# Two of 256 gathers of expert rows, each made in two transfers (120 rows and 8 rows)

## The chip, the cores and the metric

One core of one Trainium2 chip runs the whole program in one launch. The metric is the device time of a launch in microseconds, the median over several runs.

## What is computed

`x` has 256 tokens of 1024 channels. Two transformer stacks run one after the other in float32. The first has two layers (a gated mixer with neighbourhood and context attention, a convolution block, and squared-ReLU MLPs); the second has one layer: a mixer of two kinds of attention and then a feed-forward part with product-key experts. The change touches the last part, whose reference is, cut short:

```python
def peer_ffn(h, w_query, sub_keys, u_emb, v_emb):
    q = (hc @ w_query).reshape(B, T_CHUNK, PEER_HEADS, 2, PEER_DKEY // 2)
    s = jnp.einsum('bthpd,hpnd->bthpn', q, sub_keys)
    s_top, i_top = lax.top_k(s, PEER_TOPK)
    ...
    g_s, pos = lax.top_k(cand, PEER_TOPK)
    e_idx = jnp.take_along_axis(cand_idx, pos, axis=-1)
    g = jax.nn.softmax(g_s, axis=-1)
    u = u_emb[e_idx]
    act = jax.nn.gelu(jnp.einsum('btd,bthkd->bthk', hc, u), approximate=False)
    return jnp.einsum('bthk,bthkd->btd', g * act, v_emb[e_idx])
```

There are 8 heads and 16 chosen experts per head out of 16384, so each token needs 128 rows of `u_emb` and 128 of `v_emb`. The output is `x` plus this result times a gate row, with a final RMS norm.

## The kernel before

The program is written by hand for five engines, with semaphores; each engine runs its own list. VectorE is DVE, ScalarE is ACT, TensorE is PE, GpSimd is POOL and SyncE is SP in the profile.

**Gathers.** `u_emb` and `v_emb` lie side by side in one tensor `in_uv`, so that one expert is one row of 2048 floats, 8 KB. The 256 tokens are two halves of 128 (`n`), a token per partition. Gather number `g` brings one row for each of the 128 tokens of a half: half `g // 128`, head `g % 128 // 16`, choice `g % 16`. Two successive gathers are a lot (`LOTS`, `l = g // 2`), and there are 128 lots. `gather(l)` (lines 1810 to 1822) is GpSimd's list: it waits until the experts of the head are known (`s_eu`), and before each gather until the mix of the row that last used the buffer is done (`s_mix`), then issues one indirect DMA with 128 indices, one per partition, from `eu[:, h, k]` (a part of `crow`). The buffers are 10 for the first 80 gathers and 14 after that (`row_of`, line 491): two parts of `row_x`, `HID`, `row_w`, `row_h` each and six of `ring`. Every buffer has its semaphore (`s_row`), and `row_turn` (line 492) gives its value when gather `g` has landed, 16 for each transfer. From gather 84 on, gather `g` reuses the buffer of `g - 14`.

**Consumers.** For each row VectorE makes the dot with the token's `h` (`dot(l)`, line 1261, 1024 elements per partition, written over the `u` half). ScalarE takes the gelu of the two dots of a lot (line 1695), multiplies by the gates (1699) and makes two diagonal matrices (1705). TensorE adds `diag x v` to a sum in PSUM, four matmuls a row (`mix(l)`, line 2318; two calls of a 512-column matmul, each run as two). For the last two lots gelu and diagonal are made row by row (lines 1712 and 1269). Beside the dots VectorE makes the routing of later heads, 16 steps (`route_steps`; the list of experts is written at line 1245, which increments `s_eu`). Step `r` is half `r // 8` and head `r % 8`.

**End.** `finish(0)` closes the first half after lot 65, and SyncE stores output rows 0 to 127 (line 2456). `finish_last()` closes the second half, with the stores at lines 2458 and 2460.

**Elsewhere.** In the convolution block VectorE clears two borders of `yp` and waits for them with the semaphore `s_pad` (lines 896 to 898).

Of the kernel before, what the change touches and what calls it, by code (L numbers as in the profile page):

```python
# [7 lines left out]
U32 = mybir.dt.uint32  # L8
# [71 lines left out]
def program(nc, A, out):  # L80
    es = ExitStack()
    with es:
# [3 lines left out]
        def sem(name):  # L86
            return es.enter_context(nc.semaphore(name))
# [100 lines left out]
        ef = af[:, 1760:1792].rearrange("p (s k) -> p s k", s=2)  # L188
        e1 = af[:, 1792:1808]
        eu = af[:, 1808:1936].bitcast(U32).rearrange("p (h k) -> p h k", h=8)  # L190
        gates_ = On[:, 0:128].rearrange("p (h k) -> p h k", h=8)
        dots = On[:, 128:256].rearrange("p (h k) -> p h k", h=8)
        wts = On[:, 256:384].rearrange("p (h k) -> p h k", h=8)
# [120 lines left out]
        def unit_src(i):  # L314
            if not in_ring(i):
                return (late[:, 0:1024], late[:, 1024:2048], bias[:, 3072:4096], ring[:, pair_slot(L0 + 4), 0:1024])[i - W0 - 12]
            return ring[:, pair_slot(i // 2), i % 2 * 1024:i % 2 * 1024 + 1024]
# [67 lines left out]
        relu_h = Steps(sem("act_relu_hi"), [(l, s, m) for l in range(2) for s in range(8) for m in range(4)])  # L385
        relu_l = Steps(sem("dve_relu_lo"), [(l, s, m) for l in range(2) for s in range(8) for m in range(4)])
        CV, CP = (0, 1, 2, 3, 4), (5, 6, 7)
        s_pad, s_diag, s_tap, s_mean, s_cen = sem("dve_pad"), sem("act_diag"), sem("pe_tap"), sem("pe_mean"), sem("dve_centred")
        y_v, y_a = Steps(sem("dve_conv"), CV), Steps(sem("act_conv"), CP)
        s_ln, s_silu, s_yh, s_yl = sem("dve_ln"), sem("act_silu_y"), sem("act_y_hi"), sem("dve_y_lo")  # L390
        TAPS = [(kt, k) for kt in CP for k in range(31)]
# [5 lines left out]
        s_scp, s_sc2 = sem("pe_key_score"), sem("act_key_score")  # L397
        s_ngr, s_rge, s_eu = sem("dve_route_max"), sem("act_route_exp"), sem("dve_route")
        s_eu8 = sem("dve_route_first_eight")
        s_row = [sem(f"row{i}_in") for i in range(14)]  # L400
        s_dot, s_gate, s_dg, s_mix = sem("dve_dot"), sem("dve_gate_share"), sem("act_mix_diag"), sem("pe_mix")
        s_ms, s_msr, s_y, s_out = sem("dve_ms"), sem("act_ms_root"), sem("dve_y"), sem("out_done")
# [86 lines left out]
                      or 35 <= l < 40 or l >= 40 and l % 8 < 5]  # L489
        chosen_at = {route_lots[5 * (r - 1) + 2] + 1: r for r in range(1, 16)}  # L490
        row_of = [g % 10 if g < G1 else (g - G1 + 10) % NROW for g in range(256)]
        row_turn = [row_of[:g + 1].count(row_of[g]) for g in range(256)]
        row_prev = [max([p for p in range(g) if row_of[p] == row_of[g]], default=None) for g in range(256)]

        def row_in(g):
# [3 lines left out]
        row_ap = []  # L499


        def dve():
# [390 lines left out]


            have_mod(1, 2)
            ve.memset(yp[:, :, 0:15], 0.0).then_inc(s_pad, 1)
            ve.memset(yp[:, :, 271:286], 0.0).then_inc(s_pad, 1)
            V.wait_ge(s_pad, 2)
            V.then_inc(ve.tensor_tensor(ab[:, 4, :], M[:, 1, 16:24], col["bpw2"], ALU.mult))
            r = rstd("conv")  # L900
            V.wait_ge(affined.sem, affined.n)
# [864 lines left out]
        def pool():  # L1766
# [43 lines left out]
            def gather(l):  # L1810
                n, h, k0 = LOTS[l]
                if l < 4:
                    G.wait_ge(s_eu8, 1)
                else:
                    G.wait_ge(s_eu, 8 * n + h + 1)
                for i in range(2):
                    g = 2 * l + i
                    if row_prev[g] is not None:
                        G.wait_ge(s_mix, row_prev[g] + 1)
                    sm, _ = row_in(g)  # L1820
                    nc.gpsimd.indirect_dma_start(row_ap[row_of[g]], None, A["uv"],  # L1821
                                                 bass.IndirectOffsetOnAxis(ap=eu[:, h, k0 + i:k0 + i + 1], axis=0)).then_inc(sm, 16)

            G.wait_ge(s_mod, NM)
            gather(0)
# [558 lines left out]
        def sync():  # L2384
# [63 lines left out]
            for i in (L0, L0 + 1, L0 + 4):  # L2448
                for j in (2 * i, 2 * i + 1):
                    P.wait_ge(*dense[used[j]])  # L2450
                if i < L0 + 2:
                    pair(i + 4)
                else:
                    sp.dma_start(unit_src(W0 + 15), A["stream"][L0 + 7][:, 1024:2048]).then_inc(s_late[2], 16)
            P.wait_ge(s_y, 1)
            sp.dma_start(out[0, 0:128, :], xN[:, 0, :]).then_inc(s_out, 16)
            P.wait_ge(s_y, 2)
# [101 lines left out]
```

## Time and profile before

| | |
|---|---|
| median of 3 runs | 1540.09 us |
| lowest and highest | 1537.85 and 1541.22 us |
| the profiled execution's own time | 1538.54 us |
| its span, first to last instruction | 1537.2 us |
| mean granted TensorE clock | 0.992 |
| TensorE busy | 1377.1 us (90%) |
| VectorE busy | 1190.0 us (77%) |
| ScalarE busy | 721.2 us (47%) |
| GpSimd busy | 335.7 us (22%) |
| gathers: software queue | 36864 packets, 268.45 MB |

The span is shorter than the execution's own time by 1.3 us, which lie around it. Times in views are counted from the span's start. The DMA share is the mean busy share of the core's 16 DMA engines; neighbouring packets of an engine overlap a little in the records, so it can read 1.01. The name `P` in the rows is the buffer of the diagonals, `On` holds dots, weights and gates, and `cT` holds the tokens' `h`.

### The profile page before, as it was taken

What the parts mean: (1) busy time and instruction counts of PE and PEld (TensorE: products, weight loads), DVE (VectorE), ACT (ScalarE), POOL (GpSimd) and SP (SyncE); (2) the same over time, 40 slices, a digit from 0 to 9 for tenths busy, and PEclk for the clock granted to TensorE, in tenths of its full rate; (3) what the DMA queues carried; (4) which work ended last, traced back from release to release, by engine and by line L of the source; (5) the groups of instructions that cost most, each with busy time, mean ns of one, the idle gap of its engine ahead of it and who ended that gap; (6) DMA issues with size and microseconds to landing.
All of it is one profiled execution on the core that took longest, in us unless ns stands there. A gap on an engine that the chain in (4) does not pass through costs nothing.

```text
span 1537.2 us, 20250 instructions
## 1 busy us (share of the span) xinstructions
PE 1377.1 (90%) x7314; PEld 1007.4 (66%) x7314; DVE 1190.0 (77%) x2398; ACT 721.2 (47%) x1636; POOL 335.7 (22%) x312
## 2 busy tenths in 40 slices
PE   8999999999999999998999999999887687777776
PEld 3878899999997999998888844444332232223222
DVE  6977888887997788887787687777877777667655
ACT  4555565556486645555354443434433233333322
POOL 1100100001000000003110343445644254434430
PEclk9999999999999999999999999999999999999999
DMA  9764369997520499993432699999999999999995
GB/s 390 314 233 165 138 249 360 353 359 295 196 107 27 152 343 366 344 332 135 165 110 86 233 423 421 421 421 421 420 423 420 423 421 422 421 421 421 421 421 221
DMA packets 66341, 477.12 MB, mean 310 GB/s; under 512 B 7361, under 2 KB 7361, under 8 KB 9153
## 3 DMA queue, kind: packets, MB, share of 16 engines
q0 software_dynamic: 36864, 268.45, 42.0%
q1 hardware_dynamic: 29376, 207.37, 36.2%
q8 instruction: 58, 0.95, 0.2%
q14 instruction: 41, 0.34, 0.1%
q10 hardware_dynamic: 2, 0.01, 0.0%
HBM read 474.75 MB, written 1.05 MB: 310 GB/s over the span
## 4 chain that ended last, share of the span: by engine, by line
PE 52%; DMA 29%; DVE 11%; ACT 5%; issue 2%; POOL 1%; DVEq 0%; ACTq 0%; POOLq 0%
DMA ring<-in_uv,crow 11%; DMA row_x<-in_uv,crow 8%; PE ps L2318 6%; PE ps L1872 6%; PE ps L1874 5%; PE ps L1873 5%; DMA HID<-in_uv,crow 5%; PE ps L2189 4%; PE ps L2192 4%; PE ps L2191 4%; PE ps L2216 3%; PE ps L2331 2%; DVE WB L533 2%; DMA row_h<-in_uv,crow 2%; PE ps L1905 1%
## 5 line engine op out<-in xcount | busy, mean ns | idle before, releaser
L533 DVE TENSOR_TENSOR WB<-ring,WB 128x1024 fp32r<-128x1024 f32 x208 | 256.9, 1238 | 54.0 <-ACT WB L1345 51.7
L1345 ACT ACTIVATE WB<-ring 128x1024 fp32r<-128x1024 f32 x208 | 218.4, 1052 | 125.9 <-PE ps L2192 87.0
L1872 PE MATMUL ps<-hH,WB 128*128 128x256 f32 x752 | 216.6, 288 | 5.6 <-DVE WB L533 3.8
L2318 PE MATMUL ps<-ring,P 128*128 128x512 f32 x376 | 173.7, 607 | 46.5 <-ACT P L1705 46.5
L1873 PE MATMUL ps<-hL,WB 128*128 128x256 f32 x752 | 214.1, 285 | 0.0
L1874 PE MATMUL ps<-hH,WB 128*128 128x256 f32 x752 | 214.0, 285 | 0.0
L1695 ACT ACTIVATE On<-On 128x2 f32<-128x2 f32 x126 | 25.6, 203 | 369.5 <-DVE On L1261 369.4
L518 DVE CUSTOM_DVE_ANT_0 ring<-ring,crow,cols 128x1024 f32<-128x1024 f32 x128 | 163.5, 1279 | 21.1 <-DMA ring<-in_um 20.9
L2318 PEld LDWEIGHTS ps<-ring,P 128*128 128x128 f32 x376 | 68.9, 191 | 149.4 <-ACT P L1705 78.6
L1261 DVE CUSTOM_DVE_ANT_0 ring<-ring,cT 128x1024 f32<-128x1024 f32 x94 | 114.7, 1225 | 65.9 <-DMA ring<-in_uv,crow 64.0
L1872 PEld LDWEIGHTS ps<-hH,WB 128*128 128x128 f32 x752 | 145.6, 194 | 8.0 <-DVE WB L533 4.7
L2189 PE MATMUL ps<-XB,WB 128*128 128x256 f32 x512 | 145.1, 283 | 1.6 <-DVE WB L533 1.6
L1873 PEld LDWEIGHTS ps<-hL,WB 128*128 128x128 f32 x752 | 145.7, 194 | 0.1
L1874 PEld LDWEIGHTS ps<-hH,WB 128*128 128x128 f32 x752 | 145.6, 194 | 0.0
L2191 PE MATMUL ps<-XB,WB 128*128 128x256 f32 x512 | 144.9, 283 | 0.0
L2192 PE MATMUL ps<-XB,WB 128*128 128x256 f32 x512 | 144.9, 283 | 0.0
L1773 POOL TENSOR_TENSOR sq<-sq 128x256 f32<-128x256 f32 x30 | 29.3, 977 | 528.9 <-ACT sq L1350 526.9
L1821 POOL DMA_INDIRECT ring<-in_uv,crow x94 | 102.0, 1085 | 137.9 <-PE ps L2318 108.8
L2318 PE MATMUL ps<-row_w,P 128*128 128x512 f32 x160 | 75.6, 616 | 27.5 <-ACT P L1705 27.5
L2189 PEld LDWEIGHTS ps<-XB,WB 128*128 128x128 f32 x512 | 98.3, 192 | 2.0 <-DVE WB L533 2.0
L2192 PEld LDWEIGHTS ps<-XB,WB 128*128 128x128 f32 x512 | 98.3, 192 | 0.0
L2191 PEld LDWEIGHTS ps<-XB,WB 128*128 128x128 f32 x512 | 98.3, 192 | 0.0
(348 smaller groups left out, 2895.5 us busy)
## 6 DMA issues: line engine op xcount, KB each, us to landing
ring<-in_stream SPq DMA_DIRECT2D x114, 1024.0 KB, 6.7
ring<-in_um SPq DMA_DIRECT2D x66, 1024.0 KB, 7.5
ring<-in_wm SPq DMA_DIRECT2D x4, 1024.0 KB, 12.5
bias<-in_bias SPq DMA_DIRECT2D x2, 2048.0 KB, 15.4
HID<-in_um SPq DMA_DIRECT2D x4, 512.0 KB, 17.9
ring<-in_uv,crow POOLq DMA_INDIRECT x94, 27.6
xT<-in_xT SPq DMA_DIRECT2D x1, 1024.0 KB, 8.5
cT<-in_cxT SPq DMA_DIRECT2D x1, 1024.0 KB, 15.3
```

Of the source, the lines that this page charges most:

```text
L518: ve.tensor_tensor_reduce(wk, wk, crow[:, layer // 2, :], 1.0, col[f"bm{layer}"][:, m:m + 1], ALU.mult, ALU.add, M[:, layer, m:m + 1]).the ...
L533: ve.tensor_tensor(unit_dst(j, 1), unit_src(j), f(unit_dst(j, 0)), ALU.subtract).then_inc(s_lo, 1)
L1261: ins = ve.tensor_tensor_reduce(u, u, hN[:, n, :], 1.0, 0.0, ALU.mult, ALU.add, dots[:, h, k0 + i:k0 + i + 1])
L1345: se.activation(unit_dst(j, 0), unit_src(j), ACT.Copy).then_inc(s_hi, 1)
L1821: nc.gpsimd.indirect_dma_start(row_ap[row_of[g]], None, A["uv"], bass.IndirectOffsetOnAxis(ap=eu[:, h, k0 + i:k0 + i + 1], axis=0)).then_i ...
L1872: te.matmul(o, wh[:, c], hi[:, kt, :], start=(kt == 0), stop=False)
L1873: te.matmul(o, wh[:, c], lo[:, kt, :], start=False, stop=False)
L1874: mm = te.matmul(o, wl[:, c], hi[:, kt, :], start=False, stop=(kt == 7))
L2189: te.matmul(o, wh[:, c], rH[d % 2][:, k, :], start=(d == 0 and h == 0 and k == 0), stop=False, skip_group_check=True)
L2191: te.matmul(o, wh[:, c], rL[d % 2][:, k, :], start=False, stop=False, skip_group_check=True)
L2192: mm = te.matmul(o, wl[:, c], rH[d % 2][:, k, :], start=False, stop=(d == 7 and k == 3), skip_group_check=True)
L2318: mm = te.matmul(ps[4 + 2 * n + q][:, :], diag[:, g % 8, :], row_ap[row_of[g]][:, 1024 + q * 512:1536 + q * 512], start=(g % 128 == 0), st ...
```

## The change

Gathers 226 and 230 are both of the second half, head 6, choices 2 and 6, with buffers `row_x` and `row_w`. Each becomes two indirect DMAs into the same buffer: rows (partitions) 0 to 119 with their indices as before, then rows 120 to 127, whose indices are read from `eut`, on partitions 0 to 7. SyncE fills `eut` with one transfer of 8 x 16 indices from `eu[120:128, 6, :]`, once `s_eu` has reached 15. The buffer's semaphore counts 32 for such a gather. `eut` lies in a free part of `crow`. The new semaphore `s_eut` comes in, `s_pad` goes, and VectorE's own semaphore takes its place.

```diff
+        eut = af[0:8, 1936:1952].bitcast(U32)
...
-        s_pad, s_diag, s_tap, s_mean, s_cen = sem("dve_pad"), sem("act_diag"), sem("pe_tap"), sem("pe_mean"), sem("dve_centred")
+        s_diag, s_tap, s_mean, s_cen = sem("act_diag"), sem("pe_tap"), sem("pe_mean"), sem("dve_centred")
...
+        s_eut = sem("last_tokens_experts_in")
...
-        row_turn = [row_of[:g + 1].count(row_of[g]) for g in range(256)]
+        SPLIT = (226, 230)
+        row_turn = [sum((1 + (p in SPLIT)) * (row_of[p] == row_of[g]) for p in range(g + 1)) for g in range(256)]
...
-            ve.memset(yp[:, :, 0:15], 0.0).then_inc(s_pad, 1)
-            ve.memset(yp[:, :, 271:286], 0.0).then_inc(s_pad, 1)
-            V.wait_ge(s_pad, 2)
+            V.then_inc(ve.memset(yp[:, :, 0:15], 0.0))
+            V.then_inc(ve.memset(yp[:, :, 271:286], 0.0))
+            V.wait_own()
...
                     sm, _ = row_in(g)
-                    nc.gpsimd.indirect_dma_start(row_ap[row_of[g]], None, A["uv"],
-                                                 bass.IndirectOffsetOnAxis(ap=eu[:, h, k0 + i:k0 + i + 1], axis=0)).then_inc(sm, 16)
+                    n_tok = 120 if g in SPLIT else 128
+                    nc.gpsimd.indirect_dma_start(row_ap[row_of[g]][0:n_tok, :], None, A["uv"],
+                                                 bass.IndirectOffsetOnAxis(ap=eu[0:n_tok, h, k0 + i:k0 + i + 1],
+                                                                           axis=0)).then_inc(sm, 16)
+                    if g in SPLIT:
+                        G.wait_ge(s_eut, 16)
+                        nc.gpsimd.indirect_dma_start(row_ap[row_of[g]][120:128, :], None, A["uv"],
+                                                     bass.IndirectOffsetOnAxis(ap=eut[:, k0 + i:k0 + i + 1], axis=0)).then_inc(sm, 16)
...
+            h_split = SPLIT[0] % 128 // 16
+            P.wait_ge(s_eu, 8 + h_split + 1)
+            sp.dma_start(eut, eu[120:128, h_split, :]).then_inc(s_eut, 16)
             P.wait_ge(s_y, 1)
             sp.dma_start(out[0, 0:128, :], xN[:, 0, :]).then_inc(s_out, 16)
```

GpSimd's list around gathers 224 to 231, before; `pe_mix` is the wait for a buffer's last mix, `dve_route` the wait for a head's experts, and each row is one gather (x2 two alike):

```order
L1821 DMA ring<-in_uv,crow 128x2048 [waits pe_mix,dve_route]
L1821 DMA ring<-in_uv,crow 128x2048 [waits pe_mix]
L1821 DMA row_x<-in_uv,crow 128x2048 [waits pe_mix] x2
L1821 DMA HID<-in_uv,crow 128x2048 [waits pe_mix] x2
L1821 DMA row_w<-in_uv,crow 128x2048 [waits pe_mix] x2
```

And in the changed kernel:

```order
L1825 DMA ring<-in_uv,crow 128x2048 [waits pe_mix,dve_route]
L1825 DMA ring<-in_uv,crow 128x2048 [waits pe_mix]
L1825 DMA row_x<-in_uv,crow 120x2048 [waits pe_mix]
L1830 DMA row_x<-in_uv,crow 8x2048 [waits last_tokens_experts_in]
L1825 DMA row_x<-in_uv,crow 128x2048 [waits pe_mix]
L1825 DMA HID<-in_uv,crow 128x2048 [waits pe_mix] x2
L1825 DMA row_w<-in_uv,crow 120x2048 [waits pe_mix]
L1830 DMA row_w<-in_uv,crow 8x2048
L1825 DMA row_w<-in_uv,crow 128x2048 [waits pe_mix]
```

The first of the two gathers into `row_x` and the first of those into `row_w` are now a large and a small transfer each, with the gathers behind them in their old order; the first small one also waits for `eut`.

SyncE's list at the end, before, where the first row is the last load of weights and the others store the output:

```order
L2454 DMA ring<-in_stream 128x1024 [waits pe_dense]
L2456 DMA out<-xN 128x1024 [waits dve_y]
L2458 DMA out<-xN 128x512 [waits dve_y]
L2460 DMA out<-xN 128x512 [waits act_last_y]
```

And in the changed kernel:

```order
L2463 DMA ring<-in_stream 128x1024 [waits pe_dense]
L2466 DMA crow<-crow 8x16 [waits dve_route]
L2468 DMA out<-xN 128x1024 [waits dve_y]
L2470 DMA out<-xN 128x512 [waits dve_y]
L2472 DMA out<-xN 128x512 [waits act_last_y]
```

The copy of the indices and its wait for `s_eu` (`dve_route`) stand ahead of the store of the first half.

## Rows read from the trace of the kernel before

**Rows 1.** Page: busy time, the span in 40 slices, DMA queues.

```profile
PE 1377.1 (90%) x7314; PEld 1007.4 (66%) x7314; DVE 1190.0 (77%) x2398; ACT 721.2 (47%) x1636; POOL 335.7 (22%) x312
...
GB/s 390 314 233 165 138 249 360 353 359 295 196 107 27 152 343 366 344 332 135 165 110 86 233 423 421 421 421 421 420 423 420 423 421 422 421 421 421 421 421 221
...
q0 software_dynamic: 36864, 268.45, 42.0%
...
q8 instruction: 58, 0.95, 0.2%
```

**Rows 2.** Busy time by stretch: us, engines' busy time (instructions), clock, DMA share, GB/s.

```profile
880.00:980.00 100.00, 92.25 (x282) 49.71 (x280) 75.23 (x199) 42.30 (x123) 43.38 (x40) 1.00 1.01 422
...
1400.00:1500.00 100.00, 73.64 (x160) 28.55 (x159) 58.30 (x122) 30.54 (x104) 40.61 (x40) 1.00 1.01 421
```

**Rows 3.** Timeline of VectorE: first dots of two successive lots.

```profile
1444.96 1.23 DVE L1261 CUSTOM_DVE_ANT_0 ring<-ring,cT 128x1024 f32<-128x1024 f32 x1 [1.37 <-DMA ring<-in_uv,crow]
...
1449.94 1.23 DVE L1261 CUSTOM_DVE_ANT_0 ring<-ring,cT 128x1024 f32<-128x1024 f32 x1 [1.37 <-DMA ring<-in_uv,crow]
```

**Rows 4.** Groups by line, 1440 to 1519 us, VectorE's dots and TensorE's mixes.

```profile
L1261 DVE CUSTOM_DVE_ANT_0 ring<-ring,cT 128x1024 f32<-128x1024 f32 x16 | 19.6, 1225 | 20.0 <-DMA ring<-in_uv,crow 20.0
...
L2318 PE MATMUL ps<-ring,P 128*128 128x512 f32 x56 | 25.9, 605 | 9.0 <-ACT P L1705 9.0
```

**Rows 5.** Chain of waits, 1480 us to the end: start, us, what.

```profile
1498.59 28.16 DMA row_x<-in_uv,crow
...
1533.96 0.72 ACT xN L1725
```

**Rows 6.** The end by stretch, columns as in rows 2.

```profile
1510.00:1515.00 5.00, 3.72 (x10) 1.45 (x9) 2.48 (x5) 1.38 (x5) 0.00 (x0) 1.00 1.01 419
...
1516.00:1517.00 1.00, 1.00 (x4) 0.41 (x3) 0.05 (x1) 0.00 (x0) 0.00 (x0) 1.00 0.64 270
...
1518.00:1519.00 1.00, 0.15 (x1) 0.00 (x0) 0.18 (x2) 0.72 (x4) 0.00 (x0) 1.00 0.22 90
...
1520.00:1521.00 1.00, 1.00 (x4) 0.52 (x3) 0.73 (x3) 0.20 (x1) 0.00 (x0) 1.00 0.08 33
...
1522.00:1523.00 1.00, 1.00 (x4) 0.42 (x3) 1.00 (x2) 0.00 (x0) 0.00 (x0) 1.00 0.06 25
...
1524.00:1525.00 1.00, 1.00 (x3) 0.39 (x3) 0.57 (x1) 0.00 (x0) 0.00 (x0) 1.00 0.06 25
```

**Rows 7.** Timeline of VectorE, dots of rows 254 and 255, a diagonal between.

```profile
1524.43 1.23 DVE L1261 CUSTOM_DVE_ANT_0 row_x<-row_x,cT 128x1024 f32<-128x1024 f32 x1 [0.73 <-DMA row_x<-in_uv,crow]
...
1525.93 0.35 DVE L1269 TENSOR_SCALAR P<-ident,On 128x128 f32<-128x128 f32 x1 [0.27 <-ACT On L1712]
1526.78 1.22 DVE L1261 CUSTOM_DVE_ANT_0 row_x<-row_x,cT 128x1024 f32<-128x1024 f32 x1 [0.50 <-DMA row_x<-in_uv,crow]
```

**Rows 8.** Timeline of VectorE, two dots around 1433 us.

```profile
1431.44 1.27 DVE L1261 CUSTOM_DVE_ANT_0 row_w<-row_w,cT 128x1024 f32<-128x1024 f32 x1 [0.96 <-DMA row_w<-in_uv,crow]
...
1435.00 1.23 DVE L1261 CUSTOM_DVE_ANT_0 row_h<-row_h,cT 128x1024 f32<-128x1024 f32 x1 [0.27 <-DMA row_h<-in_uv,crow]
```

**Rows 9.** Timeline of TensorE, one lot of mixes.

```profile
1504.49 3.70 PE L2318 MATMUL ps<-row_w,P 128*128 128x512 f32 x8 [1.27 <-ACT P L1705]
```

**Rows 10.** Timeline of GpSimd: gathers 226 and 230.

```profile
1426.24 1.38 POOL L1821 DMA_INDIRECT row_x<-in_uv,crow  x1 [1.45 <-PE ps L2318]
...
1436.22 0.94 POOL L1821 DMA_INDIRECT row_w<-in_uv,crow  x1 [1.89 <-PE ps L2318]
```

**Rows 11.** Timeline of VectorE: the fifteenth list of experts.

```profile
1394.44 0.17 DVE L1245 CAST crow<-crow 128x16 uint32<-128x16 f32 x1
```

**Rows 12.** The output's stores: issue, and from issue to landing.

```profile
L2456 SPq DMA_DIRECT2D out<-xN x1: 348/348/348, 1220.4 to 1220.4; - x1
...
DMA to landing us min/median/max: 2.0/2.3/7.6
```

**Rows 13.** VectorE's line 899, the add behind the memsets.

```profile
L899 DVE TENSOR_TENSOR ab<-M,cols x1: 168/168/168, 380.2 to 380.2; 128x8 f32<-128x8 f32 x1
```

## The prediction

> **What bounds the kernel now.** I start with the page. TensorE is busy for 90% of the span, but that is an average over two different stages: from slice 24 of 40 on, at about 884 us, the transfer rate stands at 420 to 423 GB/s in every slice but the last [rows 1], and between 1400 and 1500 us TensorE is down to 73.64 of 100 [rows 2]. This is the stage of the gathers; they are the software queue's 36864 packets, 268 MB of the 477 MB. Then the busy time by stretch: 421 or 422 GB/s and a DMA share of 1.01 early, and again at 1400 to 1500 us, so all 16 DMA engines work without a pause [rows 2]. One gather is 128 rows of 8 KB, 1.049 MB, or 2.49 us at 421 GB/s; the 256 of them are 637 us of the 1537.2. The dots show the same beat: first dots of successive lots start at 1444.96 and 1449.94 us, 4.98 us for two gathers [rows 3].
>
> The engines that consume the rows are not the limit. Between 1440 and 1519 us VectorE waits for landings before its dots: 20.0 us in front of the 16 dots on ring rows alone [rows 4]. TensorE, with 605 ns per matmul in this view and four matmuls per row, idles 9.0 us before the ring group [rows 4]. In the chain of waits the end hangs on the last row's DMA, from its issue at 1498.59 us for 28.16 us; behind it come one dot, one mix and the closing steps, up to 1537.2 [rows 5].
>
> The decisive view is the DMA share, microsecond by microsecond, at the end [rows 6]. Until 1515 us it is 1.01. Then it falls: 0.64 between 1516 and 1517, 0.22 between 1518 and 1519, 0.08 between 1520 and 1521, and 0.06 from 1522 to 1525. One engine of 16 is 0.0625: so most engines finish their share of row 255 by 1519, a second-slowest at about 1521, and **one engine works alone for more than 5 us**, until about 1526.5. A row counts as landed only when every engine has delivered, so this one sets the dot of row 255 at 1526.78. Its last rows come at the usual beat (dots at 1524.43 and 1526.78, 2.35 us apart [rows 7]): it isn't slow at the end, it is behind. Where it fell behind shows in one place: a dot at 1431.44 is followed by one at 1435.00, 3.56 us where the beat is 2.49 [rows 8]. The page has 58 instruction packets of 16 KB on another queue (0.95 MB) [rows 1]; I take it that these pass through a particular engine and push it back about 1 us each time, which would make the lag a property of the program and not of one run. That is an inference.
>
> **The change, part by part.** (a) Gathers 226 and 230 are split into rows 0 to 119 and 120 to 127. If 120 rows are dealt 8 to an engine, 15 engines get work and one gets none. If that one is the late engine, it saves 8 rows twice, 16 x 2.49/8 = 16 x 0.311 = 4.98 us. The 36864 packets are 144 per gather, 16 more than its rows [rows 1]; for what such extra packets of the two added transfers cost I take off 0.1: **-4.9 us** at its end, 1526.5 to 1521.6. (b) The eight odd rows are dealt one each to eight engines, 0.31 us per split. These engines don't decide unless they are close to the new end: the second-slowest finishes by about 1521 and would come to 1521.6 with two added rows. So the relief is just used up, and a third split would bring next to nothing. The sum takes -4.9.
>
> Is a consumer late next? To use 4.9 us TensorE must catch up: a lot is 8 matmuls, 3.70 us of the 4.98 us beat [rows 9], so 1.28 us can be regained per lot, and four lots make 4.9 us good. From row 226 to row 255 there are 15 lots. In the last four rows dot, gelu, scaled diagonal and mix chain one another: dot start 1524.43 to diagonal end 1526.28 is 1.85 us, less than the beat of 2.49 [rows 7]. Row reuse isn't short either: the last gather is issued at 1498.59 [rows 5], and no engine has finished it before 1515 [rows 6], so over 16 us of work stand queued at each.
>
> (c) GpSimd issues two more transfers. The order view shows each of them right behind its large one. An issue takes 0.94 to 1.5 us here; gather 226 is issued at 1426.24 and 230 at 1436.22 [rows 10], GpSimd is busy 40.6 of 100 us [rows 2], and a delay of gather 227 by 1.4 us is covered by the 16 us of queue. Cost 0; without that cover it would be 2 x 1.4 = 2.8 us. (d) The eight indices are copied from partitions 120 to 127 to partitions 0 to 7 by one SyncE transfer, which waits for the fifteenth step of routing, the cast at 1394.44 [rows 11]. The trace has no such small transfer; the nearest are the stores of 256 KB (2.0 us on idle engines at best) and of 512 KB in the middle of the gathers (7.6 us) [rows 12]. I take the upper, because this one too runs in full traffic: landed by 1402.2. It is needed behind gather 226's large part, at 1427.6: 25 us of slack, cost 0 between either bound. (e) SyncE's queue: behind that new wait stands the store of output rows 0 to 127, issued at 1220.36 now [rows 12]. It moves to about 1395. Its 0.52 MB are 1.25 us of all 16 engines at either place, nothing reads them on the chip, and the end comes 140 us later: 0. (f) The two memsets and the add behind them (the add takes 168 ns at 380.2 us [rows 13]) signal on VectorE's own semaphore instead of one of their own; both wait for the same two memsets: 0.
>
> **Sum.** The profiled execution took 1538.54 us for a span of 1537.2; 1538.54 - 4.9 = 1533.6. The median of the three runs is 1540.09, 1.55 above that execution and inside their spread of 1537.85 to 1541.22. Against the median: 1540.09 - 4.9 = **1535.2 us**. 0.2% is 3.1 us, about what a measurement of this kernel can tell from no change.
>
> **Rivals.** 1. *The late engine is not the one left out.* The trace doesn't number engines. Then it keeps its 8 rows and may be among those with an extra row: 0 to +0.6 us, 1540.1 to 1540.7. For it: nothing in the rows ties the late engine to the last partitions. Against it: there are only few natural places for an omission, first or last. The Trainium skill ("DMA: Bandwidth & Descriptors", "Latency and other measured facts") says that DMA engines 7 and 15 are usually slower than the rest, by a best guess because of the software queue's descriptor rings. An omission of the last engine would fit; but the beat here is the same for the late engine as for all, and what is seen is one engine behind, not two.
>
> 2. *The omission moves on from split to split.* If shares are dealt to engines from a running position, the 120 rows skip one engine, the 8 rows begin at just that engine, and the second split skips another one, seven places on. The late engine then saves 8 - 1 = 7 rows in one split and none in the other: 7 x 0.311 = 2.2 us, 1537.9. If it is never skipped, the case is rival 1. For it: the split into 15 and 8 shares is as natural as the fixed one. Against it: no row shows either. This is the rule of the Trainium skill ("DMA: Bandwidth & Descriptors", "Why a DMA increments its semaphore by 16 and not by 1"): the number of engines is the largest up to 16 that divides the row count, taken as consecutive engines from a round-robin cursor, with an exception for some direct copies, which fill the low engines first; no run here shows which holds for gathers. By the rule the sum would be this rival's 1537.9, or that of rival 1.
>
> 3. *Slower: the eight rows travel through one engine, and it is the late one.* A transfer of few rows needn't be spread. Eight rows on one engine are 2.49 us, twice 4.98. On any other engine this stays hidden (1521 + 5.0 is still below 1526.5); only on the late one it decides, and then the end moves by up to 4.98 us: 1545.1. Against it: it takes two unfavourable dealings at once.
>
> 4. *The relief is smaller because the unprofiled runs have a smaller lag*, or the second engine is nearer: between -2 and -4, 1536 to 1538. The three runs lie around the profiled one, which speaks against a different state.
>
> **Numbers.** Full relief 0.58 (1535.2); rival 1 0.20; rival 2 with 2.2 us 0.10; rival 3 0.05; rival 4 0.07. Of full relief nearly all, and half of rival 4, is faster by over 0.2%: 0.60. Rivals 1 and 2 and the rest of 4 are within: 0.34. Slower 0.06, rival 3 and an unseen cost. The range runs from full relief with the runs' own spread of about 2 us, 1533.0, to rival 1, 1540.9; it leaves out rival 3 and the outer ends. The likeliest case's own range is 1533.0 to 1537.0.
>
> **What would show it.** Right: the stretch with a share of 0.06 at the end is gone or under 1 us, the share falls from 1.01 to 0 within some 6 us; the dots of rows 226 and 230 follow the row before at about 1.2 to 1.3 us; the last dot is at about 1521.9 and the tail behind it is still 10.4 us; GpSimd has 258 gathers with no wait for a DMA. Rival 1: the lone stretch is as long as now. Rival 2: it is 2 to 3 us shorter, with one early dot only. Rival 3: it is longer. I am wrong in the step (b) if the lone stretch goes and the time stays.

## The result, and the profile after

The changed kernel is **slower**: 1555.24 us, median of 5 runs (1553.56 to 1555.68), against 1539.22 (1536.04 to 1541.22) for the kernel before in as many runs beside it. The ratio is 1.0106, 95% interval 1.0092 to 1.0119. Forecast were 1535.2 us and a range up to 1540.9; the result lies 14.3 us above the range. The profiled execution took 1553.56 us for a span of 1552.3, 15.1 more than the span before.

The page of the changed kernel. Beside [rows 1], in the stage of the gathers (from slice 24 on) only one full slice stands out, the 38th of the transfer rates:

```profile
PE 1389.2 (89%) x7314; PEld 1013.8 (65%) x7314; DVE 1191.3 (77%) x2398; ACT 720.7 (46%) x1636; POOL 349.4 (23%) x314
...
GB/s 390 319 219 163 145 253 347 363 349 282 206 91 27 175 371 354 347 300 136 158 114 129 244 422 421 421 422 420 421 422 421 422 421 422 421 421 422 300 418 195
...
q0 software_dynamic: 36928, 268.45, 42.4%
```

The work is the same: as many matmuls, the same 268.45 MB, two GpSimd instructions more. But in one slice of 39 us the DMA engines moved 300 GB/s and not 421. The same place by stretches, and then the end (us, engines' busy time, clock, DMA share, GB/s):

```profile
1430.00:1442.00 12.00, 8.74 (x20) 3.44 (x19) 7.26 (x17) 5.13 (x14) 7.94 (x6) 1.00 1.01 419
1442.00:1454.00 12.00, 5.71 (x13) 2.31 (x12) 3.70 (x6) 2.75 (x10) 4.68 (x4) 0.94 1.02 246
1454.00:1457.00 3.00, 3.00 (x4) 1.01 (x4) 1.11 (x1) 0.00 (x0) 0.00 (x0) 0.50 1.02 377
1457.00:1469.00 12.00, 6.79 (x13) 2.43 (x11) 2.59 (x6) 1.38 (x5) 4.46 (x4) 0.90 1.03 234
1469.00:1481.00 12.00, 9.18 (x15) 3.80 (x16) 4.31 (x7) 2.75 (x10) 3.15 (x3) 0.72 1.00 391
1481.00:1520.00 39.00, 26.96 (x59) 10.36 (x58) 19.45 (x33) 11.01 (x40) 12.28 (x14) 1.00 1.01 422
1526.00:1528.00 2.00, 2.00 (x6) 0.68 (x4) 0.96 (x1) 0.00 (x0) 0.00 (x0) 1.00 0.95 397
...
1530.00:1532.00 2.00, 2.00 (x6) 0.95 (x5) 0.87 (x3) 0.00 (x0) 0.00 (x0) 1.00 0.20 82
...
1534.00:1536.00 2.00, 1.56 (x4) 0.85 (x5) 1.23 (x2) 0.87 (x3) 0.00 (x0) 1.00 0.11 45
1536.00:1538.00 2.00, 2.00 (x6) 0.80 (x6) 1.45 (x2) 0.01 (x1) 0.00 (x0) 1.00 0.07 29
1538.00:1540.00 2.00, 2.00 (x6) 0.93 (x5) 1.01 (x4) 0.20 (x1) 0.00 (x0) 1.00 0.06 25
1540.00:1542.00 2.00, 2.00 (x6) 0.77 (x5) 1.23 (x4) 0.20 (x1) 0.00 (x0) 1.00 0.04 16
```

Two stretches of 12 us, one for each split gather, have **a DMA share of 1.02 or 1.03 and only 246 and 234 GB/s**. A full share says that the engines always had a packet in hand; the packets took longer. The DMA view of 1442 to 1454 us gives their number, for the kernel before:

```profile
DMA packets 695, 5.05 MB, mean 421 GB/s; under 512 B 78, under 2 KB 78, under 8 KB 78
```

and for the changed one:

```profile
DMA packets 437, 2.96 MB, mean 246 GB/s; under 512 B 76, under 2 KB 76, under 8 KB 76
```

Leaving out the 78 and 76 small ones, 617 packets of 8 KB before and 361 now. With 16 engines x 12 us x the share, one took 16 x 12 x 1.013 / 617 = 0.315 us before, and 16 x 12 x 1.017 / 361 = 0.541 us now. And 2.96 MB is three times what the 120 rows (0.98 MB) are: the packets of the *other*, whole gathers in this stretch were slowed too. The trace's records of single packets say the same. Before, 99 of 100 row packets (8 KB) in the stage of the gathers take 0.309 to 0.322 us. In the changed kernel their mean goes from 0.313 to 0.59 us within about half a microsecond at 1442.3 us, and none of those under way between 1446 and 1450 us takes less than 0.467 us: every engine is slowed there, the late one too, which is still at earlier, whole gathers.

The end shows the second thing. The lone stretch that the change was forecast to end is still there, with a share of 0.07 to 0.06 from 1536 to 1540 us and then until the last row packet ends at 1541.3 us (1526.3 before). The late engine was not relieved.

VectorE's timeline tells which rows were late. Before, the dot of row 221:

```profile
1442.36 1.22 DVE L1261 CUSTOM_DVE_ANT_0 ring<-ring,cT 128x1024 f32<-128x1024 f32 x1 [1.15 <-DMA ring<-in_uv,crow]
```

and of row 231:

```profile
1467.24 1.22 DVE L1261 CUSTOM_DVE_ANT_0 row_w<-row_w,cT 128x1024 f32<-128x1024 f32 x1 [1.15 <-DMA row_w<-in_uv,crow]
```

In the changed kernel, rows 221, 224, 226, 230, 231 and 255:

```profile
1442.30 1.23 DVE L1264 CUSTOM_DVE_ANT_0 ring<-ring,cT 128x1024 f32<-128x1024 f32 x1 [1.13 <-DMA ring<-in_uv,crow]
...
1455.89 1.23 DVE L1264 CUSTOM_DVE_ANT_0 ring<-ring,cT 128x1024 f32<-128x1024 f32 x1 [3.62 <-DMA ring<-in_uv,crow]
...
1465.07 1.22 DVE L1264 CUSTOM_DVE_ANT_0 row_x<-row_x,cT 128x1024 f32<-128x1024 f32 x1 [4.89 <-DMA row_x<-in_uv,crow]
...
1480.39 1.23 DVE L1264 CUSTOM_DVE_ANT_0 row_w<-row_w,cT 128x1024 f32<-128x1024 f32 x1 [3.71 <-DMA row_w<-in_uv,crow]
...
1482.28 1.23 DVE L1264 CUSTOM_DVE_ANT_0 row_w<-row_w,cT 128x1024 f32<-128x1024 f32 x1 [0.66 <-DMA row_w<-in_uv,crow]
...
1541.82 1.23 DVE L1264 CUSTOM_DVE_ANT_0 row_x<-row_x,cT 128x1024 f32<-128x1024 f32 x1 [0.50 <-DMA row_x<-in_uv,crow]
```

Row 221 is in time (1442.30); for rows 222 to 230 VectorE waits up to 4.89 us. From row 231 to row 255 there are 59.54 us, 24 beats of 2.48, in both kernels. So all 15.04 us between the last dots (1541.82 against 1526.78 in [rows 7]) arise between rows 221 and 231. "From dot 221 to dot 255" is the yardstick below: **84.42 us before, 99.52 after**. It is freed of the differences that runs have in earlier stages.

The chain of waits goes through exactly these transfers:

```profile
1429.33 39.72 DMA row_x<-in_uv,crow
...
1471.55 6.11 PE ps L2327 x8
...
1477.92 29.21 DMA row_x<-in_uv,crow
...
1513.66 28.14 DMA row_x<-in_uv,crow
```

Gather 227 needs 39.72 us from issue to landing, where [rows 5] has 28.16 for a whole gather; this is 11.6 us of the 15. The eight matmuls of a lot take 6.11 us and not 3.70 as in [rows 9]: TensorE had idled for want of rows (busy for 5.71 of the 12 us before 1454) and the granted clock stood at 0.50, its lower level of 1.2 GHz, around 1455 and at 0.72 on the mean of 1469 to 1481 us. That is a consequence, and hidden: gather 241, issued at 1477.92, still takes 29.21 us to land, so work was queued.

The costs of GpSimd and SyncE I had put at nothing. GpSimd's timeline around the two small gathers:

```profile
1427.92 1.10 POOL L1830 DMA_INDIRECT row_x<-in_uv,crow  x1 [0.30 <-issue]
1429.33 1.94 POOL L1825 DMA_INDIRECT row_x<-in_uv,crow  x1 [0.30 <-issue]
...
1437.44 1.90 POOL L1830 DMA_INDIRECT row_w<-in_uv,crow  x1 [0.30 <-issue]
```

SyncE's timeline, the copy of the indices and the store behind it:

```profile
1393.40 0.76 SPq L2466 DMA_DIRECT2D crow<-crow  x1
1394.22 0.38 SPq L2468 DMA_DIRECT2D out<-xN  x1
```

The small gather follows the large one after 0.30 us of issue, with no wait for the indices, and the moved store leaves at 1394.22. Nothing waits here.

### The profile page after: what moved, and what is told of

Read it like the earlier page. It is cut to its first block, busy times and chain, and to the rows that moved or that the text cites. A ratio compares the mean times of both kernels' runs of the same rounds, so it can differ in the third digit from the quotient of the medians.

```text
span 1552.3 us, 20253 instructions
## 1 busy us (share of the span) xinstructions
PE 1389.2 (89%) x7314; PEld 1013.8 (65%) x7314; DVE 1191.3 (77%) x2398; ACT 720.7 (46%) x1636; POOL 349.4 (23%) x314
## 3 DMA queue, kind: packets, MB, share of 16 engines
q0 software_dynamic: 36928, 268.45, 42.4%
## 4 chain that ended last, share of the span: by engine, by line
PE 52%; DMA 27%; DVE 11%; ACT 5%; issue 2%; POOL 1%; another core or an unknown queue 0%; SPq 0%; DVEq 0%; ACTq 0%; POOLq 0%
DMA ring<-in_uv,crow 11%; PE ps L2327 8%; DMA row_x<-in_uv,crow 8%; PE ps L1881 6%; PE ps L1882 5%; PE ps L1883 5%; DMA HID<-in_uv,crow 5%; PE ps L2198 4%; PE ps L2201 4%; PE ps L2200 4%; PE ps L2225 3%; DMA ring<-in_um 2%; PE ps L2340 2%; DVE WB L536 2%; DMA row_h<-in_uv,crow 2%
## 5 line engine op out<-in xcount | busy, mean ns | idle before, releaser
L1825 POOL DMA_INDIRECT ring<-in_uv,crow x94 | 108.3, 1152 | 145.7 <-PE ps L2327 115.9
L2327 PE MATMUL ps<-row_w,P 128*128 128x512 f32 x160 | 79.2, 640 | 27.3 <-ACT P L1708 27.3
```

The lines of the kernel that those rows point to most:

```text
L1825: nc.gpsimd.indirect_dma_start(row_ap[row_of[g]][0:n_tok, :], None, A["uv"], bass.IndirectOffsetOnAxis(ap=eu[0:n_tok, h, k0 + i:k0 + i + 1 ...
L2327: mm = te.matmul(ps[4 + 2 * n + q][:, :], diag[:, g % 8, :], row_ap[row_of[g]][:, 1024 + q * 512:1536 + q * 512], start=(g % 128 == 0), st ...
```

## The experiments

All times are medians of 4 to 10 runs; the ratio is to the kernel before on the same chip (1539.22 us beside the changed kernel, 1538.60 beside the first four experiments, 1538.87 beside the next four, 1538.92 beside the last four). The last column is the yardstick in the one profiled execution.

| kernel | us | ratio, 95% interval | dot 221 to 255 |
|---|---|---|---|
| before | | | 84.42 |
| after | 1555.24 | 1.0106 [1.0092, 1.0119] | 99.52 |
| e1_large_only | 1553.00 | 1.0101 [1.0084, 1.0119] | 99.92 |
| e2_small_only | 1535.99 | 0.9984 [0.9974, 0.9993] | 81.05 |
| e3_copy_and_wait | 1539.31 | 1.0003 [0.9994, 1.0013] | 84.38 |
| e5_64_64 | 1550.91 | 1.0084 [1.0067, 1.0101] | 97.73 |
| e7_rows_0_63 | 1546.39 | 1.0056 [1.0035, 1.0077] | 91.59 |
| e8_rows_32_95 | 1536.84 | 0.9988 [0.9978, 0.9998] | 81.86 |
| e4_112_16 | 1551.86 | 1.0096 [1.0071, 1.0122] | 97.80 |
| e6_one_split | 1546.29 | 1.0053 [1.0034, 1.0072] | 93.49 |
| e9_large_only_early | 1545.57 | 1.0043 [1.0029, 1.0058] | 84.38 |
| e10_rows_32_91 | 1536.56 | 0.9981 [0.9971, 0.9990] | 81.93 |
| e11_32_64_32 | 1546.05 | 1.0044 [1.0027, 1.0061] | 91.03 |
| e12_last_two | 1546.55 | 1.0046 [1.0029, 1.0063] | 91.76 |

The rows shown are busy time by stretch, with the columns of [rows 2]. All diffs are against the changed kernel, that of e9_large_only_early against the one before. Where only one transfer per gather is left, `row_turn` counts one as before; `eut` and SyncE's copy into it follow the size of the second transfer.

### Which part costs: the wait and copy, the small or the large transfer

**Everything but the split** (copy of indices, wait for them, moved store, memsets; gathers whole).

```diff
-                    n_tok = 120 if g in SPLIT else 128
+                    n_tok = 128
...
-                        nc.gpsimd.indirect_dma_start(row_ap[row_of[g]][120:128, :], None, A["uv"],
...
```

> All gathers whole as before, but with the index copy on SyncE, GpSimd's wait for it at the gathers 226 and 230, the store of the first half behind the copy, and the memsets on VectorE's own semaphore. Theories A and B: 1538 to 1540.5 us, no slow stretch. Theory C: 1553 to 1556 us.

Measured: 84.38 us on the yardstick, a ratio of 1.0003, and 421 GB/s where the changed kernel has 234. Parts (d), (e) and (f) of my sum, for which I had put nothing, cost nothing. Its stretch from 1457 us:

```profile
1457.00:1469.00 12.00, 9.51 (x21) 3.91 (x22) 6.16 (x10) 2.98 (x11) 4.60 (x4) 1.00 1.01 421
```

**The large transfer alone.** Rows 120 to 127 of the two gathers are left out.

```diff
-                        nc.gpsimd.indirect_dma_start(row_ap[row_of[g]][120:128, :], None, A["uv"],
-                                                     bass.IndirectOffsetOnAxis(ap=eut[:, k0 + i:k0 + i + 1], axis=0)).then_inc(sm, 16)
```

> The changed kernel without its two small transfers: rows 120 to 127 of gathers 226 and 230 keep what an earlier gather left in the buffer (that part of the result is left out). Measured for the change: 1555.2 us, with row packets of all engines taking 440 to 680 ns instead of 309 in two stretches of about 12 us. Theory A (the 120-row transfer is dealt to the engines so that several of them write to the same group of partitions at a time, and all packets take about twice as long): both slow stretches stay, 1551 to 1555 us. Theory B (the eight rows, dealt to eight engines but all for neighbouring partitions, or the additional issue on GpSimd, are what clogs): no slow stretch, and as one engine is left out of 120 rows, 1534 to 1539 us. Theory C (the index copy, the wait for it, or the store that now stands behind it): 1553 to 1556 us, but no slow packets that belong to the gathers.

Two of its stretches:

```profile
1442.00:1446.00 4.00, 2.71 (x7) 1.06 (x6) 0.70 (x3) 1.38 (x5) 1.02 (x2) 1.00 1.01 215
...
1457.00:1469.00 12.00, 5.44 (x12) 1.97 (x10) 3.70 (x6) 1.42 (x6) 4.31 (x4) 0.93 1.03 229
```

Measured: the whole loss, +15.50 us on the yardstick, with both slow stretches, although there are no more transfers than before and 16 rows fewer. The 120-row transfer does it by itself. That also clears the second issue on GpSimd, part (c).

**The small transfer alone.** Rows 0 to 119 of the two gathers are left out.

```diff
+                    if g not in SPLIT:
+                        nc.gpsimd.indirect_dma_start(row_ap[row_of[g]][0:n_tok, :], None, A["uv"],
...
```

> The changed kernel without its two large transfers: only rows 120 to 127 of gathers 226 and 230 are brought, the other 120 rows keep what an earlier gather left (left out of the computation). Theory A: no slow stretch; 2 x 120 rows less, so up to 2 x 2.33 = 4.7 us less than before: 1534 to 1536 us. Theory B: the slow stretches stay, 1545 to 1553 us. Theory C: 1549 to 1552 us.

Two of its slow stretches:

```profile
1442.00:1446.00 4.00, 2.73 (x7) 1.06 (x6) 1.27 (x4) 1.38 (x5) 1.87 (x2) 1.00 1.03 383
...
1450.00:1454.00 4.00, 3.04 (x7) 1.44 (x8) 1.31 (x3) 1.17 (x4) 1.35 (x2) 1.00 1.06 360
```

Measured: 3.37 us gained. The late engine has at least 7 rows fewer per gather, 14 x 0.311 = 4.4 us, so some 1 us was lost; the two stretches agree, 4 x (421 - 383) / 421 + 4 x (421 - 360) / 421 = 0.94 us, and 0.3 more from 1454 to 1457 us (382 GB/s). Eight rows slow things mildly and for a short time.

### Count of rows, or their place

**Two halves of 64 rows.** With the same number of transfers, the rows divide evenly over 16 engines.

```diff
-        eut = af[0:8, 1936:1952].bitcast(U32)
+        eut = af[0:64, 1936:1952].bitcast(U32)
...
-                    n_tok = 120 if g in SPLIT else 128
+                    n_tok = 64 if g in SPLIT else 128
...
-                        nc.gpsimd.indirect_dma_start(row_ap[row_of[g]][120:128, :], None, A["uv"],
+                        nc.gpsimd.indirect_dma_start(row_ap[row_of[g]][64:128, :], None, A["uv"],
```

> Gathers 226 and 230 in two transfers of 64 rows each, 4 rows for each of 16 engines if they are dealt evenly. Theory A in the form that the partitions matter (64 neighbouring partitions are served by only half of the write paths): the packets of both transfers take about 620 ns, two slow stretches of at least 5 us, 1545 us or more. Theory A in the form that a count not divisible by 16 is dealt badly: no slow stretch, 1538 to 1540.5 us. Theory B (any second transfer): 1545 or more, theory C: 1553 to 1556.

Measured: +13.31 us on the yardstick, nearly as much. So neither a count of rows that 16 doesn't divide nor an engine left out is the cause.

**112 and 16 rows.** The same edit with 112 for 64, so that both parts divide evenly by 16, with a small second part as in the change.

> Gathers 226 and 230 in 112 and 16 rows, both multiples of 16, 7 rows and 1 row for each engine, nobody left out. Theory P: seven neighbouring partitions per engine bring several engines to one path, slow stretches as in the change, 1548 to 1556 us. Theory Q: the same. If only a count that 16 doesn't divide were dealt badly: 1538 to 1540.5 us.

Measured: +13.38 us, with 238 GB/s from 1457 to 1469 us. The same conclusion.

**Only rows 0 to 63; only rows 32 to 95.** One transfer of 64 rows each, the other 64 rows of the two gathers left out. Both have the same count, bytes and packets; the partitions differ, and with them the tokens whose experts are fetched.

```diff
+                    if g not in SPLIT:
+                        nc.gpsimd.indirect_dma_start(row_ap[row_of[g]][0:n_tok, :], None, A["uv"],
...
-                        nc.gpsimd.indirect_dma_start(row_ap[row_of[g]][120:128, :], None, A["uv"],
+                        nc.gpsimd.indirect_dma_start(row_ap[row_of[g]][0:64, :], None, A["uv"],
```

and in the second `[32:96, :]`.

> Gathers 226 and 230 bring only rows 0 to 63, to partitions 0 to 63 (the other 64 rows of each are left out). Measured: split in 64 and 64, the two gathers cost 12.3 us more than whole ones. Theory P (place: 64 neighbouring partitions from 0 use half of the write paths): packets of about 620 ns while these transfers run, and although 2 x 64 rows are missing (2.5 us of traffic) the time is 1540 to 1545 us. Theory Q (form: every gather that isn't of 128 rows is slow): the same. Theory R (two transfers for one buffer are needed for the slowness): no slow stretch, 1536 to 1537 us.

> The same with rows 32 to 95 on partitions 32 to 95; the same 64 rows, 4 for an engine, but the partitions are the lower half's second quarter and the upper half's first. Theory P: if the write path of a partition repeats at a distance of 32 partitions within a half and differs between the halves, these 64 use every path equally, so no slow stretch and 2.5 us less than before: 1536 to 1537 us. Theory Q: as rows 0 to 63, 1540 to 1545 us. Theory R: 1536 to 1537 us for both.

Busy time by stretch of the kernel with rows 0 to 63:

```profile
1442.00:1446.00 4.00, 2.73 (x7) 1.05 (x6) 0.76 (x2) 1.38 (x5) 1.16 (x2) 1.00 1.01 215
...
1457.00:1469.00 12.00, 9.16 (x20) 3.55 (x18) 5.07 (x9) 2.75 (x10) 5.90 (x5) 0.94 1.01 304
```

The same stretches of the kernel with rows 32 to 95:

```profile
1442.00:1446.00 4.00, 3.11 (x8) 1.08 (x6) 2.00 (x4) 0.76 (x4) 1.56 (x2) 1.00 1.02 424
...
1457.00:1469.00 12.00, 10.71 (x25) 4.20 (x24) 6.28 (x11) 4.14 (x15) 6.95 (x7) 1.00 1.02 423
```

This is the pair that settles it. On partitions 0 to 63 the stream falls to 215 GB/s and 7.17 us are lost, with 128 rows fewer to fetch (1546.39 us, above the 1540 to 1545 that I had expected for this case). On partitions 32 to 95 it stays at 424, and 2.56 us are gained: the eight rows that the late engine is spared, 8 x 0.311 = 2.49. **The place of the rows on the partitions decides, not their number.** That the fetched experts lie badly in memory is no rival: in the kernel before, the whole gathers 226 and 230 fetch the same rows and many more, at 421 GB/s.

The Trainium skill ("SBUF — State Buffer", "Door 1: The DMA port swizzle (why `[64,N]` ≈ `[32,N]`)") says that a DMA writes into SBUF through 16 ports, picked by bits 4 to 2 and bit 6 of the partition number. By its map partitions 0 to 63 reach only 8 of them, and partitions 32 to 95 all 16. By that rule the two kernels should differ, the first at half rate; the traces agree (215 against 424).

**60 rows, partitions 32 to 91.** 60 divides by 15 as 120 does; the other 68 rows are left out. Otherwise the edit is that of rows 32 to 95.

```diff
-                        nc.gpsimd.indirect_dma_start(row_ap[row_of[g]][120:128, :], None, A["uv"],
+                        nc.gpsimd.indirect_dma_start(row_ap[row_of[g]][32:92, :], None, A["uv"],
```

> As the run with rows 32 to 95, but rows 32 to 91: 60 rows, four each for 15 engines if the count is dealt over its largest divisor up to 16; the other 68 rows are left out. No slow stretch expected. From the dot of row 221 to the dot of row 255 it was 84.42 us before and 81.86 with rows 32 to 95. If one engine gets no row and it is the late one both times: 5 us less than before, 79.4. If it is the late one once: about 80.6. If it is never the late one: 81.9. In time: 1534, 1535.5, 1536.8 us.

Measured: 2.49 us gained and no slow stretch (424 GB/s from 1442 to 1446 us). Had the late engine been skipped once, it would have been spared four rows more, 1.2 us. It wasn't, in either transfer.

An engine *is* left out, though. The packets show it in two ways. In number, the software queue's totals fit 16 x (rows per engine + 1) packets for each transfer: 144 for 120 rows (8 for each of 15 engines), 32 for 8 rows (1 for each of 8) and 80 for 60 rows (4 for each of 15). So an engine without rows seems to get a small packet in place of each. In time, these small packets come in a burst. e1_large_only at 1440.88 to 1440.98 us:

```profile
DMA packets 20, 0.07 MB, mean 738 GB/s; under 512 B 11, under 2 KB 11, under 8 KB 11
```

and at 1460.55 to 1460.65 us:

```profile
DMA packets 13, 0.02 MB, mean 246 GB/s; under 512 B 10, under 2 KB 10, under 8 KB 10
```

In the kernel before, no stretch of 0.07 us has more than 5 small packets of this queue. The engine left out passes its empty share of gathers 226 and 230 here, at 1440.9 and 1460.6 us, while the late engine has yet to finish rows 225 and 229 (dots at 1457.65 and 1475.02). So the engine left out is not the late one, in neither of the two. The burst of the changed kernel is at 1442.3 us, just where its packets become slow; e10_rows_32_91 has its two at 1444.2 and 1455.2 us.

### How long a badly placed transfer slows the rest

**One split** (`SPLIT = (226,)`).

> Only gather 226 is split, 120 and 8; everything else as in the change. Costs that add up per split: half of the change's 16 us, so 1545.5 to 1548.5 us, one slow stretch of about 12 us. A fixed cost (copy, wait, moved store): 1553 us or more.

Its slow stretch, and the one in which the second was:

```profile
1446.00:1450.00 4.00, 0.00 (x0) 0.00 (x0) 1.15 (x1) 0.00 (x0) 1.02 (x2) 0.89 0.99 215
...
1457.00:1469.00 12.00, 6.91 (x13) 2.82 (x13) 4.74 (x9) 2.75 (x10) 2.82 (x3) 0.88 1.01 410
```

Measured: +9.07 us, one slow stretch and none at 1457 us, where the second gather's was. Each split has its own stretch, and one costs over half of two.

**The same 120-row transfers 200 gathers earlier** (kernel before; gathers 24 and 28 bring rows 0 to 119 only, the last 8 rows are left out).

```diff
+                    n_tok = 120 if g in (24, 28) else 128
-                    nc.gpsimd.indirect_dma_start(row_ap[row_of[g]], None, A["uv"],
-                                                 bass.IndirectOffsetOnAxis(ap=eu[:, h, k0 + i:k0 + i + 1], axis=0)).then_inc(sm, 16)
+                    nc.gpsimd.indirect_dma_start(row_ap[row_of[g]][0:n_tok, :], None, A["uv"],
+                                                 bass.IndirectOffsetOnAxis(ap=eu[0:n_tok, h, k0 + i:k0 + i + 1], axis=0)).then_inc(sm, 16)
```

> The kernel before, with gathers 24 and 28 (about 940 us) brought only in rows 0 to 119 (the last 8 rows left out), nothing else changed: no index copy, no second transfer. Late in the stage the same cut cost 14.4 us (e1). Theory W (while any engine works on a badly placed transfer, all engines run at half speed, so the loss is half of: own share doubled, plus the distance between the first and the last of the main group of engines, doubled): early the engines stand closer together, 1.1 us where it was 3.3, so 1.1 + 2.5 = 3.6 us per gather in place of 5.9, about 7 us in all: 1544 to 1547.5 us. Theory X (a fixed price per gather): as e1, 1551 to 1555 us.

The stretches around its two 120-row transfers:

```profile
940.00:944.00 4.00, 4.00 (x16) 2.77 (x15) 1.03 (x2) 0.38 (x1) 0.55 (x1) 1.00 1.01 215
944.00:948.00 4.00, 2.72 (x7) 0.95 (x6) 3.06 (x9) 1.38 (x5) 1.87 (x2) 1.00 0.97 260
948.00:952.00 4.00, 2.75 (x7) 0.95 (x5) 2.17 (x3) 0.00 (x0) 1.89 (x2) 1.00 1.03 412
952.00:956.00 4.00, 2.46 (x6) 1.25 (x7) 1.53 (x4) 1.38 (x5) 1.31 (x2) 1.00 1.02 268
956.00:960.00 4.00, 1.24 (x3) 0.19 (x1) 1.27 (x3) 0.00 (x0) 1.66 (x2) 0.91 1.00 221
```

Measured: +6.65 us, in the forecast range. The same transfers make slow stretches of 8 us here and of 12 us at the end. From the rows, 4 x (206 + 161 + 9 + 153 + 200) / 421 = 6.9 us of the stream are lost, and 0.7 more in the next 4 us, at 344 GB/s (the profiled execution took 1547.63 us, 2.1 above the median). The reading that I put on record and that this bears out: while any engines of the main group are inside the badly placed transfer, all of them run at about half speed, so a stretch lasts as long as the engines are spread over the queue, plus the transfer itself. Late in the program they are further apart: by the small packets with which each engine ends its share, the 16 engines of the kernel before stand on the mean 2.2 us ahead of the last one when row 24 lands (943 us), and 7.8 us when row 226 does (1455 us). That the spread is what sets the 8 and the 12 us is inferred; no run varied it alone.

**Three transfers, 32, 64 and 32 rows**, the middle one on the well placed partitions 32 to 95.

```diff
-                    n_tok = 120 if g in SPLIT else 128
+                    n_tok = 32 if g in SPLIT else 128
...
+                        nc.gpsimd.indirect_dma_start(row_ap[row_of[g]][32:96, :], None, A["uv"],
...
+                        nc.gpsimd.indirect_dma_start(row_ap[row_of[g]][96:128, :], None, A["uv"],
```

> Gathers 226 and 230 in three transfers, rows 0 to 31, 32 to 95 and 96 to 127. The middle one is well placed. Theory P for the outer ones: 32 neighbouring partitions use half of the paths, for a quarter of the rows each; with theory W two slow stretches, each half of (3.3 + 0.6 to 1.25) x 2, so 4 to 5 us per gather: 1547 to 1549 us. If the two outer transfers, which use opposite halves, run beside each other: 1539 to 1541.

Measured: +6.61 us, with 371, 283 and 320 GB/s in the three stretches from 1442 to 1454 us. That is 1 us under the 1547 to 1549 expected (1546.05 us). It is half the loss of two halves of 64, with one transfer more, so the number of transfers isn't what counts. But the two outer pieces still cost more than any relief could bring.

**The last two gathers split** (`SPLIT = (254, 255)`), where nothing is behind them to be slowed.

> The change at gathers 254 and 255 instead of 226 and 230: the other engines have nothing left to do behind them. If only the fast engines' time mattered, it would be hidden, and 1538 to 1540 us, or 1534 if the late engine is left out. Theory W: the late engine runs at half speed too while the others are at the split gathers, a common stretch of (3.3 + 5) x 2 = 16.6 us for both: up to 8.3 us lost, 1543 to 1547 us.

Its last stretches of transfer:

```profile
1515.00:1520.00 5.00, 3.70 (x8) 1.44 (x8) 1.23 (x2) 1.38 (x5) 0.00 (x0) 1.00 1.01 202
1520.00:1525.00 5.00, 0.00 (x0) 0.00 (x0) 1.23 (x2) 1.09 (x5) 0.00 (x0) 0.85 0.82 185
1525.00:1530.00 5.00, 4.95 (x6) 2.19 (x7) 1.58 (x3) 0.49 (x2) 0.00 (x0) 0.50 0.25 74
```

Measured: +7.34 us. The main group crawls to its end at about 200 GB/s while the late engine, still busy with earlier rows, is held up along with it: no row packet under way between 1516 and 1524 us takes less than 0.473 us. If it had gone on at its own rate, the slowness of the others could in part have been hidden behind its 5 us of lateness (argued; no run shows it). So even the position in which a slow large part should cost least loses.

No experiment gave a version that beats the kernel before: the three faster ones are faster by the rows that they don't fetch.

## Why the prediction was wrong

**The step that failed is (a)**, the late engine "saves 8 rows twice, 16 x 2.49/8 = 16 x 0.311 = 4.98 us". That 120 rows are dealt to 15 engines was right, by the counts of packets. But the term rested on two more things that the trace of before did not show, and both failed.

First, and worth the whole loss: the sum took 2.49/8 = 0.311 us for a row wherever the row lies. All 256 gathers before fill all 128 partitions, so this price was a price of *that* layout. In the changed kernel a packet takes 0.541 us on the mean of 1442 to 1454, on every engine in the middle of this stretch and also in whole gathers that happen to be under way. The term of the sum in place of -4.9 is +15.04. Of it, the stream itself lost 12 x (421 - 246) / 421 + 3 x (421 - 377) / 421 + 12 x (421 - 234) / 421 + 12 x (421 - 391) / 421 = 11.5 us; the other 3.5 came as the last engines fell further behind the rest: the fall of the share from 1.01 begins between 1515 and 1516 us before [rows 6] and between 1527 and 1528 after, 12 us later, and the last landing is 15 us later. Why they fell behind is not shown. I gave costs beyond the packets "0.1", and the range went only to +0.8 over the median. The bound from above that I owed was a transfer at another rate: [rows 1] has slices at 107 and 27 GB/s, but none of them with a full share, and so no row could have given this price.

The Trainium skill ("SBUF — State Buffer", "Door 1: The DMA port swizzle (why `[64,N]` ≈ `[32,N]`)") has the port map, and "DMA: Bandwidth & Descriptors", "The descriptor swizzle", has that in a transfer of 128 rows each engine writes to a port of its own. If 120 rows are dealt as 15 shares of 8 neighbouring partitions, the first four of each share lie, by that map, on 8 ports only, two engines to all but one of them, and so do the last four. That would be about half rate by the rule, an estimate from the port map, and the 120-row runs agree (215 GB/s). That the shares are neighbours is an inference; the traces don't show which engine writes where.

Second, the late engine: "if that one is the late engine" gave the 4.9 us. The lone stretch of the changed kernel ends at 1541.3 us, after a share of 0.06 to 0.07 that begins at about 1536, and so is as long as before. The bursts of small packets in e1_large_only show that another engine was left out, twice, and e10_rows_32_91 finds the late one unskipped in two further transfers. Of the rivals, the first was right on this point. In e8_rows_32_95 the price of a spared row did come out (2.56 against 2.49 us): the mechanism of relief is real where the packets keep their speed.

**What was right.** The bound: the stage is set by the DMA engines, VectorE and TensorE had slack, and every lost microsecond of the stream arrived at the end. Part (c): the delay of gather 227 by 1.10 + 0.30 us is covered; without it e1_large_only loses as much as the change. Part (d): GpSimd never waited for the indices. Parts (e) and (f): 0, by e3_copy_and_wait. The tail behind the last dot is 10.5 us, as forecast (10.4).

**What the rivals missed.** The slower case was of the wrong kind: eight rows on the late engine alone, at an unchanged price per packet (at most +5). With e2_small_only the small transfer is cleared of it. My test for step (b), "the lone stretch goes and the time stays", didn't come up. All five cases moved *shares* between engines, and none asked whether the engines' speed depends on what they write. The slowest time that any of them named was 1545.1 us.

**What stays open.** Why the packets of whole gathers and of the late engine slow down along with the badly placed ones. The Trainium skill ("DMA: Bandwidth & Descriptors", "Back-pressure in remote DMA") tells, for transfers between cores, that a saturated destination port backs up the path and stalls other engines on it. The runs here, with local gathers, look like that: in e7_rows_0_63 the transfer needs, by the Trainium skill's port map, only half of the ports, yet the whole stream halves. No run isolates it. Which engine the 120 rows leave out, by number, was not found either, only that it isn't the late one.

## What to carry to other kernels

A rate per row or per packet holds for the layout in which it was measured: before a transfer is cut, compare which partitions each piece covers, and how they are spread over the write paths, with the whole. In a saturated stream a badly placed piece isn't merely slow itself: here it halved the rate of everything in flight beside it, probably for as long as the engines took to pass through it one after another, and cost 3 to 9 us for each whole transfer of 2.5 us that was cut or cut short. When the DMA share reads 1.0 and the GB/s fall, count packets: the engines aren't short of work, each packet takes longer.

## What the hardware showed beyond expectation

- 64 rows on partitions 0 to 63 against 32 to 95: 215 against 424 GB/s at the same share.
- A transfer of 120 rows slows the queue for 8 us at 940 us and for 12 us at 1442 us of the same program.
- The queue's small packets depend on the count of rows: a gather of 128 or 64 rows has 16 of 4 bytes beside its rows, 120 or 8 rows have 24, 60 rows have 20. The engines without rows seem to get them in place of rows (from the software queue's totals: 36864 in e1_large_only are 254 x 144 + 2 x (120 + 24); 36640 in e2_small_only are 254 x 144 + 2 x (8 + 24); 36736 in e10_rows_32_91 are 254 x 144 + 2 x (60 + 20)).
- TensorE's granted clock fell to 0.50 where it was waiting for rows much of the time (busy 5.71 of 12 us), and the next eight matmuls took 6.11 us and not 3.70; with work queued at the DMA engines this cost nothing.
